# An S5 scan with its outputs one turn later, and its tables loaded and built in another order

## The reference, cut to what matters

```python
dt = exp(log_dt)[:, None]; mag = exp(lam_re * dt)
ab_re, ab_im = mag * cos(lam_im * dt), mag * sin(lam_im * dt)
bb_re = coef_re[..., None] * br - coef_im[..., None] * bim      # input matrices, 128 groups x 64 x 16
bb_im = coef_re[..., None] * bim + coef_im[..., None] * br
bu = einsum('sgc,gpc->sgp', u, bb)                              # complex
x = associative_scan(x_t = ab * x_{t-1} + bu_t)                 # 256 steps, 128 groups of 64 states
y = einsum('sgp,gcp->sgc', x_re, cr) - einsum('sgp,gcp->sgc', x_im, ci)
g = gelu(y + d_skip * h)
val, gate = split(g @ w_glu, 2); mix = val * sigmoid(gate)
```

## Time and profile before

| | us |
|---|---|
| median of 3 runs | 3343.89 (3337.52 to 3345.72) |
| the profiled execution's own time | 3343.68 |
| its span in the profile | 3341.9 |
| TensorE, VectorE, ScalarE, GpSimd busy | 3158.6, 1914.7, 1385.6, 323.4 |

### The profile page before, as it was taken

The page is one execution under the profiler, slowest core; times in us unless marked ns, Lnnn a source line. Parts: engine busy times, 40 slices in busy tenths (PEclk is TensorE's granted clock), DMA queues, the critical chain, the costliest instruction groups (busy, mean ns, idle before and its releaser), DMA issues.

```text
span 3341.9 us, 42458 instructions
## 1 busy us (share of the span) xinstructions
PE 3158.6 (95%) x16143; PEld 2638.0 (79%) x16143; DVE 1914.7 (57%) x2143; ACT 1385.6 (41%) x1883; POOL 323.4 (10%) x351
## 2 busy tenths in 40 slices
PE   8999999999999978999999999999999996968898
PEld 7887877888887767888888888878887784858786
DVE  5555569656665564555555555654465445556565
ACT  5555443444434443444343434444444453020134
POOL 2000005700008352000000000000000000000000
PEclk9999999999999957999999999999999997869899
DMA  7554576855678743666666666566676552010274
GB/s 238 172 171 150 176 196 215 250 181 191 199 223 247 230 133 120 190 213 184 195 188 189 186 193 189 183 191 188 197 219 197 169 183 98 13 41 1 65 238 151
DMA packets 312151, 580.77 MB, mean 174 GB/s; under 512 B 31976, under 2 KB 50664, under 8 KB 310176
## 3 DMA queue, kind: packets, MB, share of 16 engines
q1 hardware_dynamic: 285696, 522.85, 51.1%
q0 software_dynamic: 7696, 32.23, 3.2%
q10 hardware_dynamic: 18576, 23.12, 2.3%
HBM read 550.35 MB, written 21.50 MB: 171 GB/s over the span
## 4 chain that ended last, share of the span: by engine, by line
PE 90%; DVE 4%; ACT 2%; DMA 2%; issue 1%; ACTq 1%; POOL 0%; SPq 0%; DVEq 0%; POOLq 0%
PE acc L922 25%; PE acc L923 25%; PE acc L929 25%; PE tp L937 2%; PE acc L1440 1%; PE tp L1449 1%; PE acc L1448 1%; PE acc L1529 1%; PE acc L1536 1%; PE acc L1530 1%; PE wk L1208 1%; DMA raw<-in_mlp_w_dram 1%; DVE wL L2216 1%; DVE A L2979 1%; ACT wH L1564 0%
## 5 line engine op out<-in xcount | busy, mean ns | idle before, releaser
L2216 DVE TENSOR_TENSOR wL<-raw,wH 128x1024 fp32r<-128x1024 f32 (+1 forms) x968 | 1226.6, 1276 | 1156.7 <-ACT wH L1564 1154.6
L1564 ACT CAST wH<-raw 128x1024 fp32r<-128x1024 f32 (+1 forms) x968 | 1009.0, 1045 | 1440.0 <-PE acc L929 1260.1
L922 PE MATMUL acc<-wH,xH 128*128 128x512 f32 (+1 forms) x2208 | 870.2, 395 | 19.9 <-ACT wH L1564 15.0
L923 PE MATMUL acc<-wH,xL 128*128 128x512 f32 (+1 forms) x2208 | 859.9, 390 | 0.0
L922 PE MATMUL acc<-wH,hH 128*128 128x512 f32 x1536 | 603.2, 393 | 6.5 <-DVE hL L2270 6.5
L923 PE MATMUL acc<-wH,hL 128*128 128x512 f32 x1536 | 600.3, 391 | 0.0
L929 PE MATMUL acc<-wL,xH 128*128 128x512 f32 (+1 forms) x2208 | 589.1, 389 | 5.0 <-DVE wL L2216 5.0
L922 PEld LDWEIGHTS acc<-wH,xH 128*128 128x128 f32 x2208 | 417.5, 189 | 109.9 <-issue 12.3
L929 PEld LDWEIGHTS acc<-wL,xH 128*128 128x128 f32 x2208 | 414.3, 189 | 91.9 <-DVE wL L2216 5.8
L923 PEld LDWEIGHTS acc<-wH,xL 128*128 128x128 f32 x2208 | 417.9, 189 | 83.3
L929 PE MATMUL acc<-wL,hH 128*128 128x512 f32 x1536 | 412.1, 390 | 0.0
(11 more groups left out here) (456 smaller groups left out, 2703.0 us busy)
## 6 DMA issues: line engine op xcount, KB each, us to landing
raw<-in_mlp_w_dram SPq DMA_DIRECT2D x512, 512.0 KB, 3.8
raw<-in_w_in_dram SPq DMA_DIRECT2D x192, 512.0 KB, 3.7
raw<-in_a_w_in_dram SPq DMA_DIRECT2D x96, 512.0 KB, 3.7
raw<-in_b_w_glu_dram SPq DMA_DIRECT2D x64, 512.0 KB, 3.9
raw<-in_a_w_out_dram SPq DMA_DIRECT2D x32, 512.0 KB, 3.9
raw<-in_w_out_dram SPq DMA_DIRECT2D x32, 512.0 KB, 4.2
raw<-in_w_proj_fox_dram SPq DMA_DIRECT2D x16, 512.0 KB, 5.3
raw<-in_w_proj_rwkv_dram SPq DMA_DIRECT2D x16, 512.0 KB, 4.4
```

Source lines behind the costliest of these rows:

```text
L922: nc.tensor.matmul(bank, aH[:, k, rows], wH[:, j % SPLIT, u, 0:n], start=k == 0, stop=False)
L923: nc.tensor.matmul(bank, aL[:, k, rows], wH[:, j % SPLIT, u, 0:n], start=False, stop=False)
L1564: nc.scalar.copy(wH[:, j % SPLIT, :, 0:n], raw[:, j % RAW, :, 0:n]).then_inc(high_done, 1)
L2216: nc.vector.tensor_tensor(wL[:, j % SPLIT, :, 0:n], raw[:, j % RAW, :, 0:n], wH[:, j % SPLIT, :, 0:n].bitcast(F32), ALU.subtract).then_inc ...
```

## The change

- The scan gets 21 turns instead of 20. Outputs and gelus of a block come in turn b+4, not b+3, the transpositions in even turns from 6 on, not in odd ones from 5 on. Inputs, states, rotates, scans and combines keep their turns. SyncE's `s5_stream` is unchanged.
- The ten parameter loads go from ScalarE's queue, ahead of the MLP, to GpSimd's, after the last transposition of the MLP's input. skT is the last of them.
- The six operations of the input matrices go two and two after chunks 2, 3 and 4, not three and three after 2 and 3.
- The stores of g get semaphores of their own, so that GpSimd waits only for the buffer that it is about to overwrite.
- GpSimd clears the upper half of bpad before the masks and the lower half after them, where it waits for the store of powr.
- The loads of Tt go one behind each of the eight pieces of r, the gain behind the sixth.

```diff
--- before.py
+++ after.py
...
@@ -205,10 +205,10 @@
 def s5_steps():
 
     pe, act, dve, pool = [], [("p", 0)], [], []
-    for k in range(S5_B + 4):
-        pe += [("u0", k), ("u", k)] * (k < S5_B) + [("g", k - 1)] * (1 <= k <= S5_B) + [("y", k - 3)] * (3 <= k < S5_B + 3)
-        pe += [("h", (k - 5) // 2)] * (k >= 5 and k % 2)
-        act += [("p", k + 1)] * (k + 1 < S5_B) + [("t", k), ("d", k)] * (k < S5_B) + [("e", k - 3, 0), ("e", k - 3, 1)] * (3 <= k < S5_B + 3)
+    for k in range(S5_B + 5):
+        pe += [("u0", k), ("u", k)] * (k < S5_B) + [("g", k - 1)] * (1 <= k <= S5_B) + [("y", k - 4)] * (4 <= k < S5_B + 4)
+        pe += [("h", (k - 6) // 2)] * (k >= 6 and k % 2 == 0)
+        act += [("p", k + 1)] * (k + 1 < S5_B) + [("t", k), ("d", k)] * (k < S5_B) + [("e", k - 4, 0), ("e", k - 4, 1)] * (4 <= k < S5_B + 4)
         if 1 <= k <= S5_B:
             dve += [("rc", k - 1), ("rs", k - 1)]
         if 2 <= k <= S5_B + 1:
...
@@ -733,6 +736,17 @@
                     pool.wait_ge(s5_pool, n[0])
 
 
+                pool.wait_ge(group_done, 2 * GROUPS + len(DG))
+                pool.dma_start(sv[:, 0], I["b_a_re"][0]).then_inc(s5_in, 16)
+                pool.dma_start(sv[:, 1], I["b_a_im"][0]).then_inc(s5_in, 16)
+                pool.dma_start(sv[:, 2, 0:1], I["b_log_dt"].rearrange("o g -> g o")).then_inc(s5_in, 16)
+                for c, name in enumerate(("b_b_re", "b_b_im")):
+                    pool.dma_start(sb_b[:, c], I[name][0]).then_inc(s5_in, 16)
+                for c, name in enumerate(("b_c_re", "b_c_im")):
+                    for twice in range(2):
+                        pool.dma_start(sb_c[:, c, :, twice], I[name][0].rearrange("(k e) c p -> (e c) k p", e=8)).then_inc(s5_cin, 16)
+                pool.dma_start(skT[:], I["b_d"].rearrange("o (q p) -> (o p) q", p=P), allow_slow_non_contiguous=True).then_inc(s5_in, 16)
+
                 pool.wait_ge(s5_step, S5_STEPS)
                 pool.dma_start(bb_dram, sb_bb[:]).then_inc(s5_out, 16)
                 pool.dma_start(g_dram[:, S5_L - 1], sb_bb[:]).then_inc(s5_out, 16)
@@ -746,13 +760,14 @@
                         link(nc.gpsimd.tensor_tensor(dst[:, :, r], sb_t2[:], dst[:, :, r], ALU.add if r else ALU.subtract))
 
                 times_a(gA, sb_bb)
-                pool.dma_start(g_dram[:, 2], gA[:]).then_inc(s5_out, 16)
-                pool.wait_ge(s5_out, 48)
+                pool.dma_start(g_dram[:, 2], gA[:]).then_inc(g_out[2], 16)
+                pool.wait_ge(s5_out, 32)
                 times_a(sb_bb, gA)
-                pool.dma_start(g_dram[:, 1], sb_bb[:]).then_inc(s5_out, 16)
-                pool.wait_ge(s5_out, 64)
+                pool.dma_start(g_dram[:, 1], sb_bb[:]).then_inc(g_out[1], 16)
+                pool.wait_ge(g_out[2], 16)
                 times_a(gA, sb_bb)
-                pool.dma_start(g_dram[:, 0], gA[:]).then_inc(s5_out, 16)
+                pool.dma_start(g_dram[:, 0], gA[:]).then_inc(g_out[0], 16)
+                pool.wait_ge(g_out[1], 16)
 
                 e0 = srs[:, 1:3]
                 flip = 0
...
@@ -794,8 +809,7 @@
                                 pool.dma_start(bT[:, r, :, twice], bb_dram.rearrange("(k e) c r s -> r (e c) k s", e=8)[r]).then_inc(s5_bin, 16)
                 assert n[0] == S5_TURNED, n[0]
                 pool.dma_start(p_dram, powr[:]).then_inc(powr_out, 16)
-                pool.wait_ge(powr_out, 16)
-                link(nc.gpsimd.memset(bpad[:], 0.0))
+                link(nc.gpsimd.memset(bpad[:, S5_HP:], 0.0))
                 link(nc.gpsimd.memset(choose[:], 0.0))
                 for m in range(MT):
                     part = choose[:, m].rearrange("p (h a i) -> p h a i", h=2, a=MT)[:, :, m]
@@ -804,6 +818,9 @@
                         link(nc.gpsimd.affine_select(out=part, in_=part, compare_op=ALU.is_ge, fill=0.0, base=base,
                                                      pattern=[[0, 2], [step, 32]], channel_multiplier=-1 if step > 0 else 1))
                 assert n[0] == S5_CHOSEN
+                pool.wait_ge(powr_out, 16)
+                link(nc.gpsimd.memset(bpad[:, 0:S5_HP], 0.0))
+                assert n[0] == S5_CLEAR
                 for h in range(2):
 
                     pool.wait_ge(s5_step, S5_POWERS[h])
@@ -814,15 +831,8 @@
                 pool.wait_ge(powers_out, 32)
                 pool.wait_ge(kernels_out, 32)
                 pool.dma_start(powr[:], p_dram).then_inc(powr_in, 16)
-                pool.dma_start(gain[:], norms[2].broadcast_to([P, D])).then_inc(gain_in, 16)
                 nc.gpsimd.memset(Tt[:], 0.0).then_inc(toep_clear, 1)
                 pool.wait_ge(toep_clear, 1)
-                for g in range(2):
-                    for e in range(S5_L):
-                        rows = slice(64 * g + 16 * e, 64 * g + 16 * e + 16)
-                        src = k_dram.rearrange("h q (a g c) n -> g c (h q a) n", a=4, g=2)[g][:, :, 0:(S5_L - e) * S5_C]
-                        pool.dma_start(Tt[rows, :, e * S5_C:], src).then_inc(toep_in, 16)
-
                 pool.wait_ge(powr_in, 16)
                 sh = [P, 8, 8, 8]
                 four = lambda t: t.rearrange("p a (h l) -> p a h l", h=8)
@@ -839,6 +849,12 @@
                         link(nc.gpsimd.tensor_tensor(tb, hi[1], lo[1 - c], ALU.mult))
                         link(nc.gpsimd.tensor_tensor(four(tmade[:, b, :, c]), ta, tb, ALU.add if c else ALU.subtract))
                     pool.dma_start(r_dram[:, pairs], tmade[:, b]).then_inc(phases_out[b], 16)
+                    g, e = i // S5_L, i % S5_L
+                    rows = slice(64 * g + 16 * e, 64 * g + 16 * e + 16)
+                    src = k_dram.rearrange("h q (a g c) n -> g c (h q a) n", a=4, g=2)[g][:, :, 0:(S5_L - e) * S5_C]
+                    pool.dma_start(Tt[rows, :, e * S5_C:], src).then_inc(toep_in, 16)
+                    if i == 5:
+                        pool.dma_start(gain[:], norms[2].broadcast_to([P, D])).then_inc(gain_in, 16)
 
                 for b in range(2):
                     pool.wait_ge(phases_out[b], 16 * 4)
@@ -1239,15 +1255,15 @@
                         SPE.mark(s_pe, last, "h", j)
                 last.then_inc(group_done, 1)
 
-            for k in range(S5_B + 4):
+            for k in range(S5_B + 5):
                 if k < S5_B:
                     inputs_of(k)
                 if 1 <= k <= S5_B:
                     states_of(k - 1)
-                if 3 <= k < S5_B + 3:
-                    outputs_of(k - 3)
-                if k >= 5 and k % 2:
-                    mixed_turn((k - 5) // 2)
+                if 4 <= k < S5_B + 4:
+                    outputs_of(k - 4)
+                if k >= 6 and k % 2 == 0:
+                    mixed_turn((k - 6) // 2)
             t.group += GROUPS
 
             def mixed_ready(j):
...
@@ -1841,18 +1855,6 @@
                 lead_high(c - 1)
                 split(c0 + c + 1, 0)
 
-            def s5_load():
-
-                act.dma_start(sv[:, 0], I["b_a_re"][0]).then_inc(s5_in, 16)
-                act.dma_start(sv[:, 1], I["b_a_im"][0]).then_inc(s5_in, 16)
-                act.dma_start(sv[:, 2, 0:1], I["b_log_dt"].rearrange("o g -> g o")).then_inc(s5_in, 16)
-                act.dma_start(skT[:], I["b_d"].rearrange("o (q p) -> (o p) q", p=P), allow_slow_non_contiguous=True).then_inc(s5_in, 16)
-                for c, name in enumerate(("b_b_re", "b_b_im")):
-                    act.dma_start(sb_b[:, c], I[name][0]).then_inc(s5_in, 16)
-                for c, name in enumerate(("b_c_re", "b_c_im")):
-                    for twice in range(2):
-                        act.dma_start(sb_c[:, c, :, twice], I[name][0].rearrange("(k e) c p -> (e c) k p", e=8)).then_inc(s5_cin, 16)
-
             def s5_scalars(c):
 
                 if c == 0:
...
@@ -2566,14 +2568,19 @@
                     link(nc.vector.tensor_tensor(pks[:, 2, twice], sn, sv[:, 17], ALU.mult))
                 assert n[0] == S5_PHASES
 
-            def input_matrices(c):
+            def input_matrices(n):
 
                 wide = [P, S5_P, S5_C]
                 cr, ci = sv[:, 15].unsqueeze(2).broadcast_to(wide), sv[:, 16].unsqueeze(2).broadcast_to(wide)
-                o = sb_bb[:, :, c].rearrange("p c s -> p s c")
-                link(nc.vector.tensor_tensor(o, cr, sb_b[:, c], ALU.mult))
-                link(nc.vector.tensor_tensor(sb_t[:], ci, sb_b[:, 1 - c], ALU.mult))
-                link(nc.vector.tensor_tensor(o, o, sb_t[:], ALU.add if c else ALU.subtract))
+                for i in (n, n + 1):
+                    c = i // 3
+                    o = sb_bb[:, :, c].rearrange("p c s -> p s c")
+                    if i % 3 == 0:
+                        link(nc.vector.tensor_tensor(o, cr, sb_b[:, c], ALU.mult))
+                    if i % 3 == 1:
+                        link(nc.vector.tensor_tensor(sb_t[:], ci, sb_b[:, 1 - c], ALU.mult))
+                    if i % 3 == 2:
```

(3 more changed lines are left out.)

34 lines of the change are left out of this document (16 added, 18 removed).

## The result

The kernel became faster: 3302.78 us as the median of four runs (3304.29, 3277.89, 3303.28, 3302.28) against 3342.27 before, a ratio of 0.9873 with a 95% interval of 0.9825 to 0.9921. The prediction was 3314.5 with a range of 3301 to 3329: faster, as forecast, and 12 us more so. The profiled execution took 3304.29. Its span is 3302.6 us where it was 3341.9, which before rounding is 39.4 us less.

What follows compares the result with a forecast made beforehand. The prediction took TensorE, busy 95% of the span, as the bound and looked for its waits in the first MLP and S5 scan. Gains 18 + 4.5 - 1 + 7.7 = 29.2 us gave 3314.5 us, range 3301 to 3329.

Steps and rivals of the forecast that it cites:

- the pair of turns: S5 scan loop: two turns, one with h, would fall from 13.62 to 12.0 us, TensorE's own work.
- the new stop of part 2: First MLP near 440: late data from GpSimd's load burst would stop TensorE for 4 us, bounds 0 and 8.
- Part 3: Input matrices over chunks 2 to 4: 6 us won at hL, 7 lost beside GpSimd's table, together -1 us.
- Part 1: S5 scan: outputs one turn later would gain 18 us, bounds 11 and 26.
- the round trip through x: S5 scan: VectorE's scan, GpSimd, TensorE's y, ScalarE and VectorE's hL set the pace; TensorE idles 1.62 us before y.
- The clock rival: Scan: TensorE returns to 2.4 GHz, VectorE bounds the pair at some 10.4 us; time 3306, chance 0.17.
- The tail: End of the S5 scan: last rotate to first GLU matmul would stay at 16.5 us.
- The new rings: Scan: new waits between engines from the later outputs would cost nothing; a rival gave them 3333 us, chance 0.06.
- Part 2: First MLP near 440: small loads issued by GpSimd instead of ScalarE would gain 4.5 us, bounds 0 to 8.4.
- the prediction's criterion: Beside GpSimd's table: the prediction is wrong if TensorE's waits for wL sum to more than 15 us.
- Part 4: First MLP near 1030: Tt loads spread between the tables would remove a 6.1 us stop, gaining 7.7 us.
- neither hurts: First MLP: neither the load burst nor the backlog beside the table costs time; gain 40 us, 3304, chance 0.10.

Runs made afterwards that it cites:

- e1: Kernel before the change with only the scan's later outputs added (turn b+4 instead of b+3): 3316.74 us against 3338.15, ratio 0.9931.
- e2: Changed kernel with outputs, gelus and transposes back in their old turns: 3323.26 us, ratio 0.9956 to the kernel before.
- e7: Kernel before with TensorE's idle time in the scan filled by unused transposes of the identity: 3329.38 us against 3339.28, ratio 0.9975.
- e8: Changed kernel with unused transposes filling TensorE's idle time in the scan and ahead of the norm's scale: 3292.11 us, ratio 0.9885 to the kernel before.
- e3: Changed kernel with the ten small parameter loads back on ScalarE's queue: 3311.61 us, ratio 0.9920 to the kernel before.
- e9: Changed kernel with two more 512 KB transfers ahead of GpSimd's ten small loads: 3283.61 us in a single run.
- e6: Changed kernel with the eight Tt loads and the gain back in one burst ahead of the tables: 3313.02 us in a single run.
- e4: Changed kernel with the input matrices three and three after chunks 2 and 3, GpSimd's waits as changed: 3304.42 us, ratio 0.9882 to the kernel before.
- e5: Changed kernel with GpSimd's two waits for the stores of g as before: 3297.42 us, ratio 0.9869 to the kernel before.

## Why the prediction was right and wrong

Two terms of the sum were off by most: the pair of turns, forecast at 12.0 us and measured at 10.5 (4.3 us of the result), and the new stop of part 2, forecast at 4 us and not there (4.4 us of the result). Part 3 was off by 2.8 us the other way.

**Part 1: right in the mechanism, the pair mis-sized.** The prediction found the round trip through x, and said that TensorE would no longer wait for it on its way. The changed kernel, e1 and e2 give 22.3, 22.8 and 20.8 us against the 18 forecast. The step that failed is "So the pair falls to TensorE's own work, 13.62 - 1.62 = 12.0 us": it took TensorE's durations at 1.2 GHz as given. The clock rival said otherwise and got the row right, VectorE as the bound, "some 10.4 us"; measured are 10.5. It got 17%, and it is what happened in every trace of a kernel with later outputs. The argument against it, the reading of 0.50 from 1220 to 1230, came from a loop that waited 1.62 us in every pair, and that wait was what the change removed. e7 shows the tie: filled, the same old loop runs at 2.4 GHz for parts of the time. How much idle time brings the clock down isn't shown: the loop after has a spell of 2.07 us before y too, and its clock goes up and down. A duration measured at one clock can't be carried over to a loop whose idle time is gone.

By the Trainium skill (TensorE: Matmul & The Clock Gate, The HAM clock gate) sustained activity releases the throttle; e7 and e8 agree, with windows at 1.00 where the unfilled kernels have 0.50 to 0.66. If activity is read as the busy share, e2 does not agree: its TensorE is busy 7.6 to 9.8 of every 10 us from 1170 to 1250, at 0.50 throughout.

VectorE's own work in a pair was taken as 9.6 us and is 10.5, since two of its operations got slower beside a busier GpSimd (the views by line and shape; first before, 1215:1255, then after, 1197:1232; busy us, mean ns, idle before):

```profile
L2716 DVE TENSOR_TENSOR rc<-rc 128x256 f32<-128x256 f32 x12 | 10.9, 947 | 0.0
L2724 DVE TENSOR_TENSOR_SCAN rc<-dd,rc 128x256 f32<-128x256 f32 x12 | 7.8, 692 | 0.0
```

```profile
L2722 DVE TENSOR_TENSOR rc<-rc 128x256 f32<-128x256 f32 x13 | 13.7, 1092 | 0.0
L2730 DVE TENSOR_TENSOR_SCAN rc<-dd,rc 128x256 f32<-128x256 f32 x13 | 11.2, 897 | 0.0
```

Four combines and scans a pair are 4 x (145 + 205) ns = 1.4 us more, less what merged rows overlap: about the 0.9 that was missing. That it is GpSimd can be read inside one trace: of the scans before (1185 to 1280), 18 have next to nothing of GpSimd beside them and take 673 ns on average, 4 lie wholly beside one of its operations and take 1380. After, 5 take 659 and 8 take 1136, and GpSimd is beside 67% of a scan's time instead of 25%. The rotates, which read TensorE's wk in PSUM, take 0.68 or 0.69 us with and without it. The hand-overs that I had allowed for are not there.

The tail was forecast at 16.5 and is 17.3. The new rings (t behind y, zc behind y, rt on SyncE's queue) cost nothing, as argued. What stays open is whether the new order would run at 12.0 us a pair if the clock stayed low; no run kept it low through the turns with h. The first turns do stand at 0.50, and there y follows y in 5.41 us (1176.82 to 1182.23) without a wait, where the prediction had 5.6 for a turn without h. With its 6.4 for the turn with h that would make 11.8 us, an estimate, so TensorE would set the pace at the low clock.

**Part 2: the gain right, the new stop wrong.** The wH wait and its clock were 8.4 us in the prediction, and 8.9 and 8.3 us (e3) on the chip. The stop of 4 us that was to take its place didn't come. ScalarE's timeline after, and the landings of 415:460 (count, KB, median us):

```profile
437.46 1.05 ACT L1580 CAST wH<-raw 128x1024 fp32r<-128x1024 f32 x1 [5.59 <-DMA raw<-in_mlp_w_dram]
442.32 1.05 ACT L1580 CAST wH<-raw 128x1024 fp32r<-128x1024 f32 x1 [3.81 <-DMA raw<-in_mlp_w_dram]
```

```profile
sb_c<-in_b_c_im_dram POOLq DMA_DIRECT2D x2, 512.0 KB, 16.7
skT<-in_b_d_dram POOLq DMA_DIRECT2D x1, 8.0 KB, 18.3
```

The data did come late: 3.92 + 2.14 = 6.1 us of lateness, of the size that the two bursts in the trace had suggested. The failed step is the last one: "I take 4, the middle" priced a stop, when the lateness had first to be set against the 6.7 us of cover that the same part had just read. 6.1 - 6.7 is no stop; in e9 6.9 gives one of 0.7. The margin is thin: e6 has the same loads at this place, its three late casts add up to 0.82 + 2.66 + 3.01 = 6.5 us by the same count, and there TensorE stopped for 1.7 us. So the count is good to a us or two. The two bounds, 0 and 8, did hold.

The rule of the Trainium skill that was weighed (DMA: Bandwidth & Descriptors, Rules for kernel authors), that DMAs on another queue save issue time alone, is borne out: TensorE won 8.9 us of the 13.35 of issue time, the weights came 6.1 us late, and the DMA shares from 430 to 440 and 440 to 450 are still 1.05 and 0.87, where they were 1.02 and 1.18.

**Part 3: -1 forecast, -3.8 measured.** The stop at hL went with its clock, 6.4 us (6 forecast). Beside the table the spacing was as read, seven splits in 23.45 us:

```profile
539.15 23.45 DVE L2218 TENSOR_TENSOR wL<-raw,wH 128x1024 fp32r<-128x1024 f32 x7
```

The waits sum to 5.7 (forecast 6.9), but TensorE lost 10.2 us. The clock of 560 to 600 is 0.96, so 3.2 us ran at 1.2 GHz and 1.6 us were lost; the other 2.9 us are not in the list of waits. Matmuls start 0.227 us apart here, but each is recorded with 0.39, so the idle time before a matmul is listed 0.16 us too short; the matmul behind it comes 0.11 late as well. Seven such stops and three too short for the list make 2.7 us by the starts. So the prediction's criterion, the sum of waits, read too little; the difference of starts reads it all. e4 and e5 divide the cost: spreading the matrices is worth 0.4 to 0.6 us without the pauses and 1.6 with them, and the two pauses are worth 5.4. The prediction had the direction ("The change drops both pauses"). Its step that failed is the 4 us that it gave back "for the two short issue gaps": one such gap, at 554.85, lies inside the seven splits above, and they took 3.35 us each all the same. GpSimd's products beside them show why it gives nothing back:

```profile
541.56 3.27 POOL L760 TENSOR_TENSOR gA<-sb_t,gA 128x1024 f32<-128x1024 f32 x1
544.91 3.28 POOL L758 TENSOR_TENSOR sb_t<-sv,sb_bb 128x1024 f32<-128x1024 f32 x1
```

They come every 3.35 us too. One split passes with each product, and the gap of 0.9 us is shorter than the 1.23 that a split takes alone. Without the 4 us the forecast would have been a stop of 10.9 us; TensorE lost 10.2.

**Part 4: right.** 7.7 forecast, 8.5 measured, 7.9 by e6.

**The sum.** 22.3 + 8.9 - 3.8 + 8.5 = 35.9 where 29.2 was forecast; 0.7 more lies ahead of the MLP and 2.8 behind 1300, where the kernels don't differ. The result sits near the rival "neither hurts", 3304, but not by its mechanism, since the backlog beside the table did hurt. Two cases held at once, the high clock and the harmless burst, and the prediction had given no chance to both together, though they have nothing to do with each other. 26 - 1 + 8.4 + 7.7 = 41 would have been 3302.6, just above the lower end of its range of 3301 to 3329, and so is the result.

## What to carry to other kernels

- Where a change removes TensorE's idle time, work the new time out at both clock levels and look which engine bounds at each; a low clock in the trace of before may be the effect of the very wait that goes.
- A late operand costs what it is later than the cover of its buffers. Read the lateness from the idle time before each cast, add it up over the casts in a row, and subtract the cover before a stop is priced.
- Two engines that slow each other down need slack between them: two pauses of 4.7 us in GpSimd's table were worth 5.4 us to TensorE. And independent rivals deserve a chance together.
